# One norm where two stood between the blocks, and a pooled input moved in among the gates

## The reference, cut to what matters

```python
def first_block(x, ...):
    h = x
    for l in range(2):
        h = hybrid_layer(h, ...)      # ends with: x + merged @ w_out
    return rmsnorm(h, final_g)        # the last norm of block 1

def second_block(x, meta_tokens, ...):
    h = concatenate([meta_tokens, x])           # 16 + 1024 = 1040 rows
    for l in range(2):
        u = rms_norm(h, norm_w[l]) @ w_in[l]    # l = 0: the first norm of block 2
        f_in, f_gate, p_in, p_gate, c_q, c_kv, k_r, a_gate = split(u)
        y_f = fourier_mix(f_in)
        y_p = pool_mix(p_in)      # windowed means over the sequence, minus p_in, times a matrix
        y_a = mla_mix(c_q, c_kv, k_r)
        mix = concatenate([y_f * silu(f_gate), y_p * silu(p_gate), y_a * silu(a_gate)])
        h = h + mix @ w_out[l]
    return rms_norm(h, final_norm_w)[16:]
```

## Time and profile before

| | |
|---|---|
| median of 3 runs | 4044.62 us (4043.38 to 4048.3) |
| the profiled execution | 4042.67 us |
| its span, first to last instruction | 4040.9 us |
| mean granted TensorE clock | 0.964 of full speed |
| TensorE busy with matmuls | 3743.9 us, 93% of the span |
| VectorE, ScalarE, GpSimd busy | 1718.9, 1265.5 and 1091.6 us |

### The profile page before, as it was taken

The page is one execution under the profiler, slowest core; times in us unless marked ns, Lnnn a source line. Parts: engine busy times, 40 slices in busy tenths (PEclk is TensorE's granted clock), DMA queues, the critical chain, the costliest instruction groups (busy, mean ns, idle before and its releaser), DMA issues.

```text
span 4040.9 us, 51127 instructions
## 1 busy us (share of the span) xinstructions
PE 3743.9 (93%) x20820; PEld 3311.2 (82%) x20820; DVE 1718.9 (43%) x3136; ACT 1265.5 (31%) x2868; POOL 1091.6 (27%) x806
## 2 busy tenths in 40 slices
PE   6999998999999899999899999968988998898898
PEld 5787777888887788777778888858988998898898
DVE  6624554433325552455443332554334334333333
ACT  3212443034331211244313333122245422134541
POOL 2533222321113362322231221326310023530002
PEclk9999999999999999999999999979989999998999
DMA  3111110401114212111130112322100031110012
GB/s 113 37 68 63 35 50 32 147 31 42 42 40 176 87 42 78 47 40 44 42 141 29 42 40 79 130 83 65 43 26 19 20 108 56 60 52 13 14 41 95
DMA packets 85195, 243.91 MB, mean 60 GB/s; under 512 B 10720, under 2 KB 25312, under 8 KB 84960
## 3 DMA queue, kind: packets, MB, share of 16 engines
q1 hardware_dynamic: 84960, 240.64, 17.4%
HBM read 190.07 MB, written 50.53 MB: 60 GB/s over the span
## 4 chain that ended last, share of the span: by engine, by line
PE 70%; DVE 14%; ACT 7%; issue 5%; DMA 2%; POOL 2%; SPq 1%; DVEq 0%; POOLq 0%; ACTq 0%
PE pj L1212 27%; PE pS L1212 21%; PE po L1420 4%; PE po L1311 4%; PE pS L1400 3%; PE pS L1402 2%; DVE tmp L2030 1%; PE pS L1282 1%; DVE KK L2042 1%; PE pS L1283 1%; PE pt L1298 1%; DVE tmp L2033 1%; ACT PT L1612 1%; PE pj L1386 1%; DVE tmp L2027 1%
## 5 line engine op out<-in xcount | busy, mean ns | idle before, releaser
L2471 POOL TENSOR_SCALAR Whi<-stage 128x1024 fp32r<-128x1024 f32 (+4 forms) x272 | 277.8, 1021 | 2138.9 <-DMA stage<-wstream 1328.4
L1212 PE MATMUL pj<-Hhi,Whi 128*128 128x512 f32 x1648 | 657.5, 399 | 8.3 <-DVE Hlo L1901 3.3
L1212 PE MATMUL pj<-Hhi,Wlo 128*128 128x512 f32 x1648 | 645.5, 392 | 0.0
L1212 PE MATMUL pj<-Hlo,Whi 128*128 128x512 f32 x1648 | 645.0, 391 | 0.0
L2473 POOL TENSOR_TENSOR Wlo<-stage,Whi 128x1024 fp32r<-128x1024 f32 (+4 forms) x272 | 621.9, 2287 | 22.7
L1212 PEld LDWEIGHTS pj<-Hhi,Whi 128*128 128x128 f32 x1648 | 311.6, 189 | 76.3 <-ACT PT L1612 6.6
L1212 PEld LDWEIGHTS pj<-Hhi,Wlo 128*128 128x128 f32 x1648 | 311.0, 189 | 66.8
L1212 PEld LDWEIGHTS pj<-Hlo,Whi 128*128 128x128 f32 x1648 | 311.6, 189 | 61.4
L1212 PE MATMUL pS<-Hhi,Whi 128*128 128x512 f32 x784 | 312.7, 399 | 12.2 <-DVE Hlo L1901 5.1
L1212 PE MATMUL pS<-Hlo,Whi 128*128 128x512 f32 x784 | 310.0, 395 | 0.0
L1212 PE MATMUL pS<-Hhi,Wlo 128*128 128x512 f32 x784 | 309.5, 395 | 0.0
(11 more groups left out here) (389 smaller groups left out, 7735.8 us busy)
## 6 DMA issues: line engine op xcount, KB each, us to landing
stage<-wstream SPq DMA_DIRECT2D x228, 512.0 KB, 4.3
merged<-Mb SPq DMA_DIRECT2D x32, 512.0 KB, 2.9
Mb<-merged SPq DMA_DIRECT2D x32, 512.0 KB, 5.1
gates<-tmp SPq DMA_DIRECT2D x48, 256.0 KB, 2.2
TH<-gates SPq DMA_DIRECT2D x24, 512.0 KB, 6.1
xres<-X SPq DMA_DIRECT2D x16, 520.0 KB, 5.7
xr<-xres SPq DMA_DIRECT2D x16, 520.0 KB, 4.6
X<-xT SPq DMA_DIRECT2D x16, 256.0 KB, 6.8
```

The source lines that it names most:

```text
L1212: x = pe.e.matmul(ps, w[a][:, v.koff + k * P:v.koff + k * P + P], moving(v.of, b, k, v.t0, v.n), start=k == 0 and i == 0, stop=k == v.K - ...
L2471: pool.e.tensor_scalar(upper, stage, 1.0, 0.0, ALU.mult, ALU.add).then_inc(*pool.tick("whi", c))
```

## The change

- Block 1's last norm and block 2's first become one. `output1` squares each residual tile twice on ScalarE, once as it is and once times the gain (`square("g")`), and VectorE sums both (`acc`, `accg`). `last_sums` makes the factor of a token from both sums. `row_spread` brings it back; the 16 meta tokens have their own sum (`sqm`) and their own gain, so `norm2` scales 16 and 332 columns apart in the first chunk.
- X stays unscaled. It is stored to `xres2` tile by tile in the output layer (`last_out`), with the loads of the meta tokens and of block 2's tables ahead of that layer (`tables2_in`). In `output2` of block 2's first layer each reloaded tile is scaled on VectorE (`residual2_in`).
- In both layers of block 2, `norm2` stops after the first chunk; the norms of the second and third chunk stand around the first products. f0, f1 and p0 also go together in the second chunk, f0 and f1 in the third. The seven small loads come after the phase mark, and the parts made of them after the copies of those products.
- `pool1` is cut in two: its sums on GpSimd (`pool1_sums`) stand right behind the Fourier products, its end on VectorE and ScalarE between `gate_p(0)` and the second `gate_f`.
- Weight loads are now placed by a rule (each behind the last use of the buffer that it needs). Tiles move in memory so that nothing overlaps.

The core of the diff (the functions of each engine that are only renamed or regrouped, and the addresses, are left out):

```diff
-        for u, upto in self.upto:
-            last = min(upto, len(self.weights) - 1)
-            u["loads"] = range(loaded, last + 1)
-            loaded = max(loaded, last + 1)
+        at, behind = 0, [None] * len(self.units)
+        for u in reversed(self.units):
+            behind[u.id] = at
+            if u.kind in ("proj", "dft", "values_in", "first_weights"):
+                at = u.id
+        at = 0
+        for c in range(len(self.weights)):
+            at = max(at, self.first[c].id if c < NR else behind[self.used_at[c - NR]])
+            self.units[at].setdefault("loads", []).append(c)
...
+        last = l + 1 == DEPTH
+        if last:
+            self.put("tables2_in")
         for e in range(8):
+            if last and e == 1:
+                meta = self.put("meta_squares")
             r = self.put("residual_in", l=l, e=e, ring=e % 2, ring_free=ring_free[e % 2],
                          stored=self.resready[e] if self.resready else None)
             box = {}
@@ -792,15 +816,19 @@
                                   opens=i == 0, ends=i == 1, ready=self.h_ready[i], banked=True, emptied="residual",
                                   e=e, xo=xo, res_in=("res_in", r.id)))
                 self.square("1", e, i, t0, n, ("residual", u.id), xo)
+                if last:
+                    self.square("g", e, i, t0, n, ("residual", u.id), xo)
                 self.x_ready[i].append(("residual", u.id))
                 if e == 7:
                     self.h_free.append(("proj", u.id))
                     if i == 0:
-                        sums = self.rstd("1", [self.accs[0]], D, 0, within=True)
+                        sums = self.last_sums(0, meta.id) if last else self.rstd("1", [self.accs[0]], D, 0, within=True)
                     else:
-                        u["inside"] = {3: [sums]}
+                        u["inside"] = {4 if last else 3: [sums]}
             ring_free[e % 2] = ("residual", u.id)
-            if l + 1 < DEPTH:
+            if last:
+                self.put("last_out", e=e, ready=("residual", u.id))
+            else:
                 x = self.put("residual_out", e=e, ready=("residual", u.id))
                 self.restok.append(("res_out", x.id))
         self.resready = self.restok
...
+    def last_sums(self, c, meta):
+        u = self.put("last_sums", c=c, accs=[self.accs[c], self.accs["g", c]], meta=meta, po_free=self.po_free, within=True)
+        self.po_free = ("last_mean", u.id, 1)
+        return u
     def between(self, sums):
-        ph = self.phase()
-        rs = self.spread(sums) + self.spread(self.rstd("1", [self.accs[1]], D, 1))
-        u = self.put("between", rs=[("rs", x.id) for x in rs], x_ready=self.x_ready[0] + self.x_ready[1])
-        self.accs = {0: ("accs", u.id)}
-        self.phase()
-        u = self.put("between_out", of=u.id)
-        self.restok = [("res2", k) for k in range(8)]
-        self.resready = self.restok
-        self.x_ready = [[("meta_in", k) for k in range(8)] + [("final1", 7)]] * 3
+        power = ("power", sums.id, 0)
+        self.rs = [self.row_spread("RS2", 0, [(49, META)] + [(45 + i, P) for i in range(3)], power)]
+        self.x_ready = [self.x_ready[0] + [("meta_in", k) for k in range(8)], self.x_ready[0] + self.x_ready[1], self.x_ready[1]]
+        self.half_sums = sums
+        self.restok = [("res2", 6), ("res2", 7)]
+        self.resready = self.restok * 4
...
-        of = self.norm_of("2", 8, 60 + 8 * l, [None] * 4, ())
+        of = self.norm_of("2", 8, 60 + 8 * l if l else 98, [None] * 4, ())
         of["x"] = "X2" if l else "X"
-        self.upto.append((self.put("first_weights"), len(self.weights) + NR - 1))
+        of["meta"] = None if l else 60
+        self.put("first_weights")
         self.inside = {}
         self.norm(of, 0, range(2), rs[0], self.x_ready[0], self.h_free)
-        if len(rs) < 3:
+        if l == 0:
+            other = self.last_sums(1, None)
+        elif len(rs) < 3:
             other = self.rstd("2", [self.accs[2]], D, 2, within=True)
         self.norm(of, 0, range(2, 8), rs[0], self.x_ready[0], self.h_free)
-        if len(rs) < 3:
+        if l == 0:
+            power = ("power", other.id, 0)
+            rs = rs + [self.row_spread("RS2", 400, [(48, P)] + [(76 + i, P) for i in range(3)], power, within=True),
+                       self.row_spread("RS2", 912, [(79, P)], power, within=True)]
+            self.inside = {0: [other], 4: rs[1:]}
+            self.half_sums = [self.half_sums, other]
+        elif len(rs) < 3:
             rs = rs + self.spread(other, within=True)
             self.inside = {0: [other], 3: [rs[2]]}
-        for c in (1, 2):
+        self.h_ready = self.norm_ready(of)
+        def rest(c):
             self.norm(of, c, range(8), rs[c], self.x_ready[c], self.h_free)
-        self.h_ready = self.norm_ready(of)
-        self.phase()
+        return rest
...
+        f = [self.in2("f_copy", key("f", i), x=i, box={}, emptied="f_copy") for i in range(2)]
+        p = [self.in2("p_copy", key("p", i), x=i, box={}, emptied="p_copy") for i in range(2)]
+        for c in range(3):
+            for u in (f[0][c], f[1][c], p[0][c]):
+                u["ph"] = ph
+        norm(1)
+        self.together([f[0][0], f[1][0], p[0][0]], self.inside)
+        norm(2)
+        self.phase()
+        if l == 0:
+            self.y_free = self.ph + self.restok
+        else:
+            self.ph = self.ph + self.resready
+        self.put("small_dma", l=l)
+        self.together([f[0][1], f[1][1], p[0][1]], {})
+        self.together([f[0][2], f[1][2]], {})
+        self.add(p[0][2])
+        f_ready = [("f_copy", f[i][2].id) for i in range(2)]
+        ph = self.ph
         self.put("small_in", l=l)
-        f = [self.in2("f_copy", key("f", i), x=i, box={}, emptied="f_copy", ahead=NR - 1 - i) for i in range(2)]
-        p = [self.in2("p_copy", key("p", i), x=i, box={}, emptied="p_copy", ahead=i * (NR - 1)) for i in range(2)]
-        self.together([f[0][0], f[1][0], p[0][0]], self.inside)
-        for c in (1, 2):
-            self.run([f[0][c], f[1][c], p[0][c]])
-        f_ready = [("f_copy", f[i][2].id) for i in range(2)]
...
         self.bank_free[2:6], self.banks = ps_free, WIDE
+        levels = self.put("pool1_sums", l=l, p_ready=p_ready[1], z_ready=z_ready)
         x = self.put("mark3").id
...
+        gate_f(0)
         gate_p(0, z_ready)
-        u = self.put("pool1", l=l, p_ready=p_ready[1], z_ready=z_ready, z_free=z_free[0], a_ready=a_ready)
+        u = self.put("pool1", l=l, levels=levels.id, z_free=z_free[0], a_ready=a_ready)
+        gate_f(1)
         gate_p(1, [("lo", u.id, 1)])
...
+        if l == 0:
+            for c, col in enumerate((41, 72)):
+                u = self.row_spread("RSy", 512 * c, [(col + i, P) for i in range(4)], ("power", self.half_sums[c].id, 0))
+            scaled = ("rs", u.id)
...
+    def residual2_in(u):
+        if u.scaled:
+            x = m.xr2[u.ring][:, META:L2]
+            dve.wait_ge(("res2_in", u.id))
+            dve.wait_ge(u.scaled)
+            phase_met(u)
+            STT(out=x, in0=x, scalar=vec[:, 52 + u.e:53 + u.e], in1=m.RSy[:, :], op0=ALU.mult, op1=ALU.mult).then_inc(
+                *dve.tick("res2_scaled", u.id))
...
+    def last_out(u):
+        sp.wait_ge(u.ready)
+        sp.wait_ge(("meta_in", u.e))
+        START(t["xres2"][u.e, :, :], m.X[:, u.e, :]).then_inc(*sp.landing(f"t{u.e % 2}", "res2", u.e))
```

More of the change, by code:

```diff
@@ L154, in memory @@
     m.sq = [at(f"sq1{i}", o + 2048 * i, [P, 512]) for i in range(2)]; o += 4096
+    m.accg = at("accg", s1, [P, S])
+    m.sqg = [at(f"sqg{i}", s1 + 4096 + 2048 * i, [P, 512]) for i in range(2)]
+    m.sqm = at("sqm", s1 + 8192, [P, 8, META])
     o = y0
@@ L196, in memory @@
-    m.osb = [at(f"osb{i}", o + 1056 * i, [P, 264]) for i in range(2)]; o += 2112
-    m.edge = at("edge", o, [P, 2, 16]); o += 128
+    m.fe = (at("fehi", s2, [P, 2, 2, LP], F32R), at("felo", s2 + 10240, [P, 2, 2, LP], F32R))
+    m.Fy = at("Fy", s2, [P, 2, L2])
+    m.z = (at("zhi", s2 + 8320, [P, L2], F32R), at("zlo", s2 + 12480, [P, L2], F32R))
+    a0, a1 = s1 + 12416, s1 + 33664
+    m.A = (at("Ahi", a0, [P, 5, 512], F32R), at("Alo", a1, [P, 5, 512], F32R))
+    m.SG = at("SG", a0, [P, L2])
@@ L328, in add @@
         if u.opens:
-            u.box["c"] = self.weight(u, u.key, u.ahead)
+            u.box["c"] = self.weight(u.key)
         if u.box is not None:
             u["c"] = u.box["c"]
+            if u.ends:
+                self.used_at[u.c] = u.id
         if u.banked:
@@ L361, in take, with weight @@
         return b, self.bank_free[b]
-    def weight(self, u, key, ahead=None):
+    def weight(self, key):
         self.weights.append(key)
-        i = len(self.weights) - 1
-        self.upto.append((u, i + (NR - 1 if ahead is None else ahead)))
-        return i
+        return len(self.weights) - 1
     def phase(self):
@@ L434, in first_block @@
         self.put("load_x", i=0)
```

(32 more changed lines are left out.)

199 lines of the change are left out of this document (97 added, 102 removed).

## The result

| | before | after |
|---|---|---|
| median of the runs, us | 4045.98 (4043.38 to 4048.3) | 4015.76 (4009.26 to 4020.9) |
| ratio | | 0.9926, 95% interval 0.991 to 0.9941 |
| profiled execution, us (span) | 4042.67 (4040.9) | 4009.26 (4007.5) |

The change makes the kernel 30 us faster, not the 49 us forecast, and the time lies above the range. Between the two profiled executions it is 33.4 us, against a sum of 49.2. The table shows where the other 15.8 us are. Both executions are cut at matmuls that they have in common: the first matmul of block 1's last output layer, the end of its last one, the first matmul of the fold (`po<-fc,fc`, whose input the small loads bring) in either layer of block 2, and the first of block 2's first output layer. All times are in us, and the last column is what the prediction's sum has for the stretch.

The account below looks back on a forecast made before the run. TensorE, busy 93% of the span, was taken as the bound. Terms -36.6 - 5.2 + 0.5 - 15.0 + 2.4 + 2.6 + 0.7 + 1.4 = -49.2 took 4042.67 to 3993.5 us; forecast 3994, range 3983 to 4008.

Parts of the forecast that it names:

- The boundary: Between blocks 1 and 2: merged norm shortens the hole, net -36.6 us; tables made later in the first layer, +0.5.
- k = 2: Third input tile of H2 at the block boundary: starts 15 us after block 1's last matmul instead of 52.7.
- The gates: Second pooled input moved earlier in both layers of block 2: waits for zlo and clock losses go, -15.0 us.
- my margin: In the gates: GpSimd's moved work delays ScalarE and VectorE, but six PSUM banks cover it by about 1.5 us.
- Fx: Block 2's second layer: copies ahead of the small loads remove a 3.7 us wait and its clock loss, -5.2 us.
- Neither costs: Block 1's last output layer: added squares and sums, and loads delaying the first residual by some 4 us, cost nothing.
- the forecast +5.0: Block 1's last output layer, all at e = 7: longer sums +2.4 us and TensorE waiting for late accg +2.6.
- I charged one: Sums exposed to GpSimd's weight splits: only the one on the path, accg at e = 7, was priced, +2.6 us.
- 2.4 more: End of block 1's last output layer: first-half sums have 32 passes instead of 8, +2.4 us.
- Only the last matters: Block 2's first output layer: scaling each residual tile costs only at the last one, e = 7, +1.4 us.
- VectorE is held by GpSimd in more places: Rival, chance 0.12: accg, e = 7's scaling and norm tiles each lose 2.1 us; four places on the path give 4002.
- The rival on the other side: Block 1's last output layer becomes VectorE's at 8.4 us a tile, +48 us, eating the gain; chance 0.01.

Follow-up runs that it names:

- experiment 3: The changed kernel with residual rows of block 1's last output layer asked for one step earlier, ahead of the previous step's store: 4005.69 us, ratio 0.9906.
- the kernel of 6: The changed kernel with residual rows one step earlier in block 1's last and block 2's output layers, and alternating slots for squares: 3989.71 us, ratio 0.9868.
- experiment 4: The changed kernel without the scaling of the residual in block 2's first output layer (it computes something else): 4004.58 us, ratio 0.9906.

## Why the prediction was wrong, point by point

**The boundary: right.** -34.6 us against -36.6 + 0.5. In the other profiled executions with this boundary and p0's weight behind the store it is 48.7 to 49.9 us long, against 84.5 before. Most of the difference lies in k = 2, which comes 1.3 us later. I had it wait for VectorE until 15.0, but no VectorE row stands on that part of the chain: TensorE itself is longer, with 1.24 us for p0's three matmuls (0.9), 3.21 for the sums of 16 passes (2.7) and 2.82 for k = 1 (2.0), all at half clock. The row spread took 1.11 (I had 1.1).

**The gates: right, and 15.0 is near the upper end.** -8.6 and -9.9 against -7.5 each, no wait for `zlo`, and 15 us lost by the ratios when undone. TensorE nowhere waits in the gates for ScalarE or VectorE: my margin held. But this execution flatters them. In the ten with the pooled input early the first stretch takes 515.9 to 520.7 us, the second 626.6 to 630.0 (the changed kernel's second execution: 520.1 and 629.4), against 524.6 and 636.2 in the mean of three of before with their variants: -6.6 and -7.1.

**Fx: nearly.** The wait of 3.7 us is gone. The stretch from the end of the layer's last matmul to the second fold went from 50.8 to 47.1 us: -3.6, not -5.2. In all eleven executions that have this part of the change it takes 46.3 to 47.4, in the three without it 50.8 to 52.9, which is -5.0 in the mean.

**Block 1's last output layer: wrong, and this is the step that failed first.** I wrote "Neither costs" of the squares and sums beside the products. I had compared them with TensorE's 10.9 us as if they were free to slide. They are links of the ring that experiment 3 shows, which passes through the store and the next row's load. I even read in the earlier trace rows that a store holds up the load, and used it for e = 7 only; block 1's last layer had no store before, and now has one at every step. Four executions with the rows early take 93.5 to 95.6 us (+3.6 to +5.7 against before: the forecast +5.0; one of them is without the second squares; a fifth, with p0's weight moved too, took 96.4), five with the rows late and both sums 98.5 to 101.6. The mechanism that I missed is worth 6 us. Its second half is that GpSimd's split meets VectorE's second sum not once, but in the first chunk of every step from e = 2 on. VectorE's timeline, then GpSimd's:

```profile
2595.73 1.40 DVE L1966 TENSOR_TENSOR acc<-acc,sq 128x512 f32<-128x512 f32 x1 [0.70 <-ACT sq L1561]
2597.05 2.88 DVE L1966 TENSOR_TENSOR accg<-accg,sqg 128x512 f32<-128x512 f32 x1
...
2607.01 1.42 DVE L1966 TENSOR_TENSOR acc<-acc,sq 128x512 f32<-128x512 f32 x1 [0.70 <-ACT sq L1561]
2608.35 2.88 DVE L1966 TENSOR_TENSOR accg<-accg,sqg 128x512 f32<-128x512 f32 x1
```

```profile
2595.54 1.05 POOL L2571 TENSOR_SCALAR Whi<-stage 128x1024 fp32r<-128x1024 f32 x1 [5.71 <-DMA stage<-wstream]
2596.68 2.71 POOL L2573 TENSOR_TENSOR Wlo<-stage,Whi 128x1024 fp32r<-128x1024 f32 x1
...
2606.84 1.05 POOL L2571 TENSOR_SCALAR Whi<-stage 128x1024 fp32r<-128x1024 f32 x1 [7.46 <-DMA stage<-wstream]
2607.98 2.70 POOL L2573 TENSOR_TENSOR Wlo<-stage,Whi 128x1024 fp32r<-128x1024 f32 x1
```

`accg` takes 2.88 us instead of 0.69, each time until half a us behind the end of `Wlo`. That this repeats seems no chance: the weight's load stands in SP's queue right behind the row's, X starts at 2594.34 and `Whi` at 2595.54, and the ring would keep the two in step. I read this from the rows and tested no other order of the loads. In numbers of rows alone: 2.88 - 0.69 = 2.2 us of the ring's 11.57, and without it the ring would be 9.4 by this estimate, shorter than TensorE's step. The rule of the Trainium skill that the prediction set beside the earlier trace rows (SBUF — State Buffer, "Who interferes with whom") says that every such sum is exposed; I charged one. The rows here agree with the rule: the sums that start inside a split are held, and X, which has one input in PSUM, takes 0.69 us each time.

At e = 7 the sums of 32 passes took 3.55 + 0.51 = 4.06 us, at a granted clock of 0.50 after TensorE had stood still for 5.8. That is 3.3 more than the 0.79 of before, where I had 2.4 more. In the kernel of 6 the wait ahead of them was 1.4 us, the granted clock was 1.00 during the first 2.4 us of them, and they took 2.40, 1.6 more than before.

**Block 2's first output layer: wrong for the same reason.** "Only the last matters" I wrote of the scaling, and priced it at 1.4 us. There is the same kind of ring, and the scaling (1.30) is a link of it at every step. From the changed kernel's chain:

```profile
3287.22 0.53 DVE X L2390
...
3288.30 2.72 DVE acc L1966
...
3292.54 0.44 DVE X L2390
3292.99 0.32 SPq L2786
3293.35 4.89 DMA xr<-xres
3298.27 1.30 DVE xr L2314
...
3299.66 0.53 DVE X L2390
```

That is 12.4 us from X to X, and TensorE needs 11.4 (24 matmuls at 0.158, three times). The step without a long hold is shorter here too: the one from 3311.79 to 3321.64, whose first sum took 0.52 us and not 2.7, went round in 9.85. So the lag seems to need both the scaling and the held sum, but only the scaling was taken away by itself (experiment 4). The layer got 5.7 us longer here and 8.1 in the mean of five executions, against 2.1 forecast (0.7 and 1.4).

**The start: no step of mine at all.** I priced the three places that the change is about, and not the line of `square` that the whole kernel uses. It costs 3.8 to 3.9 us at the first matmul. Some of it comes back by 71 us: eight profiled executions with fixed slots stand 0.7 to 3.7 us behind before there, five others with alternating ones between 2.9 us ahead and 0.2 behind.

**What is left of the +8.3** is a drift of 5 us between 1910 and 2150 us, in code that no edit touches. Five of fourteen profiled executions have it (3.5 to 5.1 us), the changed kernel's two among them. The last section has what is known of it; its cause stays open. Sum of the misses in this execution: 8.3 + 4.4 + 1.5 - 1.1 + 5.2 - 2.4 = 15.9, by the table (15.8 but for rounding). The failed step explains the 4.4 and 3.6 of the 5.2 (5.7 less the 2.1 forecast), that is 8.0 us; the other 1.6 are those of Fx, and the 8.3 are the slots and the drift.

Of the rivals, "VectorE is held by GpSimd in more places" was the nearest, but the two profiles show the holding as part of a ring and not as four separate places. The rival on the other side had the right layer, and I judged it by a tile's work and not by the ring's length.

## What to carry to other kernels

Ahead of saying that added work "lies beside" the products, follow one turn of the loop from an instruction to the same one in the next step, over queues and transfers too, and compare that with the bounding engine's step; here, what was added to a link counted at every step as soon as the ring was the longer one. The cure that worked here is to take the transfer out of the ring by asking for the data a step earlier, ahead of the store that waits: the two earlier loads together made 0.9887 of 0.9926 to 0.9935, 16 to 19 us, more than half of what the change itself gave. And a line that moves in a shared helper is to be priced at every caller.

## What the runs showed of the hardware

The same instructions took up to 5 us longer in some executions, and the granted clock goes with it. Windows of the changed kernel and then of experiment 3 (which has the same code there and is 2 us ahead):

```profile
1960.00:1990.00 30.00, 25.72 (x140) 21.77 (x139) 18.02 (x42) 15.20 (x39) 6.38 (x10) 0.94 0.00 1
```

```profile
1960.00:1990.00 30.00, 26.45 (x154) 22.69 (x155) 15.80 (x36) 15.64 (x40) 6.38 (x10) 1.00 0.03 10
```

The first had a part of this stretch at 1.2 instead of 2.4 GHz, ran 140 matmuls instead of 154, and the waits `pj <- tmp` of the whole passage are 4.6 us instead of 2.2. All fourteen profiled executions divide in this way: the five with the drift have a mean granted clock of 0.87 to 0.89 from 1960 to 1975 us and of 0.89 from 1995 to 2010, the nine without it 1.00 in both. What decides between the two, and whether the clock is the cause, I could not tell; the medians of the changed kernel (4015.76 and 4017.87) may contain it or not as it falls. A difference of one profiled execution below 5 us is therefore no evidence by itself here.

After the boundary's idle time the half clock lasted through the sums and until about 2684.4, 9.9 us after p0's first matmul (granted clock 0.50): three matmuls then take 0.54 us instead of 0.87. In the kernel of 6 it lasted 9.9 us there too (2658.89 to 2668.77). The prediction had taken 4.5 us from the earlier trace rows. And 16 passes of the sums took 3.21 us in that stretch, but 1.92 at e = 7 in the kernel of 6, at full clock.
